# Routing rewritten: choices by tile, one strided operation, blocks by rounding, expert 0 first, first gathers borderless; condition loaded first

## What is computed

```
c_act = silu(c)
mod = c_act @ w_mod + b_mod                       # 1024 -> 6 x 1024
sh1, sc1, gt1, sh2, sc2, gt2 = split(mod, 6)
h = rms_norm(x, g_norm1) * (1 + sc1) + sh1
u = h @ w_in ; attention over q, k, v ; conv branch over ga, gb
x = x + gt1 * (concat(attn, conv) @ w_out)
h2 = rms_norm(x, g_norm2) * (1 + sc2) + sh2
x = x + gt2 * hier_moe(h2)

hier_moe: grp = argmax over 4 group logits; top 2 of the 8 expert logits of that group
          weights = softmax(top 2) * softmax(group logits)[grp]
          the 1024 assignments sorted by expert, each expert padded to whole blocks of rows
          y = (silu(xb @ w_gate[e]) * (xb @ w_up[e])) @ w_down[e]   for each block
```

## Time and profile before

| | us |
|---|---|
| median of three runs (2045.68, 2050.49, 2052.24) | 2050.49 |
| the profiled execution | 2045.59 |
| its span | 2044.0 |
| PE busy in the span | 1875.2 (92%) |
| DVE busy | 1243.2 (61%) |
| ACT busy | 1005.9 (49%) |

### The profile page before, as it was taken

The page is one execution under the profiler, slowest core; times in us unless marked ns, Lnnn a source line. Parts: engine busy times, 40 slices in busy tenths (PEclk is TensorE's granted clock), DMA queues, the critical chain, the costliest instruction groups (busy, mean ns, idle before and its releaser), DMA issues. The chain is left out here.

```text
span 2044.0 us, 28612 instructions
## 1 busy us (share of the span) xinstructions
PE 1875.2 (92%) x10635; PEld 1540.7 (75%) x10635; DVE 1243.2 (61%) x1673; ACT 1005.9 (49%) x1461; POOL 118.1 (6%) x159
## 2 busy tenths in 40 slices
PE   3999895899999999993799989989999989999997
PEld 1883443788888888883785569988999779899886
DVE  3865555799998999996435546734225554544333
ACT  3423421788887888884455653345332333322322
POOL 1001000111111111111100000000000000000000
PEclk8999996899999999997899999989999999999999
DMA  8856912899999999997111011112233113232321
GB/s 301 277 187 186 374 35 103 314 384 387 388 377 379 388 393 396 387 364 251 49 52 43 1 42 42 42 42 84 83 104 104 63 52 104 85 102 84 123 83 41
DMA packets 116101, 372.67 MB, mean 182 GB/s; under 512 B 8175, under 2 KB 70917, under 8 KB 102695
## 3 DMA queue, kind: packets, MB, share of 16 engines
q1 hardware_dynamic: 108566, 348.08, 46.5%
q0 software_dynamic: 7072, 23.13, 3.4%
q10 hardware_dynamic: 370, 0.14, 0.0%
HBM read 333.09 MB, written 33.82 MB: 180 GB/s over the span
## 5 line engine op out<-in xcount | busy, mean ns | idle before, releaser
L1444 DVE TENSOR_TENSOR parts_memory<-fixed,parts_memory 128x1024 fp32r<-128x1024 f32 x384 | 443.1, 1219 | 47.9 <-ACT parts_memory L1396 46.4
L1396 ACT ACTIVATE parts_memory<-fixed 128x1024 fp32r<-128x1024 f32 x384 | 375.0, 1066 | 38.7 <-DMA fixed<-in_w_exp_gate_dram 37.9
L1658 PE MATMUL psum<-parts_memory 128*128 128x256 f32 (+3 forms) x1136 | 345.6, 304 | 9.5 <-PEq L1875 3.3
L1659 PE MATMUL psum<-parts_memory 128*128 128x256 f32 (+3 forms) x1136 | 341.8, 301 | 0.0
L1660 PE MATMUL psum<-parts_memory 128*128 128x256 f32 (+3 forms) x1136 | 341.7, 301 | 0.0
L1557 DVE TENSOR_TENSOR parts_memory<-fixed,parts_memory 128x1024 fp32r<-128x1024 f32 x139 | 166.9, 1221 | 217.4 <-ACT parts_memory L1549 217.3
L1658 PEld LDWEIGHTS psum<-parts_memory 128*128 128x128 f32 x1136 | 216.6, 191 | 19.3 <-DVE parts_memory L1557 4.6
L1659 PEld LDWEIGHTS psum<-parts_memory 128*128 128x128 f32 x1136 | 216.8, 191 | 7.0
L1660 PEld LDWEIGHTS psum<-parts_memory 128*128 128x128 f32 x1136 | 216.7, 191 | 6.9
L1658 PE MATMUL psum<-mix_parts,parts_memory 128*128 128x256 f32 (+2 forms) x664 | 206.4, 311 | 4.7 <-PEq L2579 4.0
L1326 PE MATMUL psum<-parts_memory,token_parts 128*128 128x512 f32 x512 | 206.1, 403 | 2.8 <-DVE parts_memory L1444 2.8
(11 more groups left out here) (422 smaller groups left out, 2888.2 us busy)
## 6 DMA issues: line engine op xcount, KB each, us to landing
fixed<-in_w_exp_gate_dram SPq DMA_DIRECT2D x32, 2048.0 KB
fixed<-in_w_exp_up_dram SPq DMA_DIRECT2D x32, 2048.0 KB, 10.5
fixed<-in_w_exp_down_dram SPq DMA_DIRECT2D x32, 2048.0 KB, 9.9
fixed<-in_w_in_dram SPq DMA_DIRECT2D x36, 1024.0 KB, 5.4
expert_rows<-fixed SPq DMA_DIRECT2D x8, 2560.0 KB, 25.5
fixed<-in_w_mod_dram SPq DMA_DIRECT2D x8, 2048.0 KB, 10.8
fixed<-in_w_ffn_up_dram SPq DMA_DIRECT2D x11, 1024.0 KB, 5.3
fixed<-in_w_ffn_gate_dram SPq DMA_DIRECT2D x11, 1024.0 KB, 5.3
```

Source lines behind the costliest of these rows:

```text
L1396: act.activation(weights[:, 0, piece, :], ring[:, s, q * PIECE:(q + 1) * PIECE], ACT.Copy).then_inc(high_ok, 1)
L1444: dve.tensor_tensor(out, src, high_part.bitcast(F32), ALU.subtract).then_inc(done, 1)
L1658: pe.matmul(out, x(0), w(0), start=start, stop=False)
L1659: pe.matmul(out, x(0), w(1), start=False, stop=False)
```

## The change

- The condition c is loaded by itself and first; PE turns it alone, so that silu(c) and the products with it wait for c and no longer for all parameters. The parameters are turned behind the fourth `mod`, and ACT copies them behind the root.
- `idle_products` are products of constants into a bank that nobody reads: one behind each of the last four `mod(k)`, two behind the turn of the mod rows, three behind the rank products and three at the end of the routing.
- In the attention stage ACT writes sh2 and sc2 with their channels already permuted, so that only one operation by half tile, x times sc2, reads with a stride; it no longer needs the norm. The root takes scale and eps with it (`eps_col`), which removes DVE's variance step, and the norm comes in with sh2 in one fused operation by half tile.
- PE's order puts route(t-1) into the middle of the second half of a tile's mix and turn(t-1) behind the first half; DVE chooses for tile t-1 (`choose`) between the two halves of tile t.
- Group logits are padded to eight with -1e30, which saves a copy. Blocks come by rounding: adding 1.5 * 2^30 in fp32 rounds to a multiple of 128. The one-hot is written in halves. Weights of the choices, block counts and the list of experts are computed behind the table.
- The first block is always expert 0's (`least` gives it at least 128 rows), so its weights are loaded without waiting for a result: down at the start of the stage, gate and up behind the last mix.
- The first two gathers move from the expert stage into the routing stage, right behind the table, with all 128 rows and no branch. In the expert stage ACT and DVE split the first gate weights ahead of the first tokens.

The diff, cut to its core:

```diff
@@ input_projection
             pe.wait_ge(built, 4)
-            pe.wait_ge(params, 16 * n_params)
-            for i, (rows, n) in enumerate(((rows1, N_COLS + 16), (rows2, TAPS * CM), (rows3, 3 * FM))):
-                pe.transpose(psum[:, i, 0:n], rows[0:n, :], ident[0:n, 0:n]).then_inc(cols_ps, 1)
+            pe.wait_ge(c_in, 16)
+            pe.transpose(psum[:, C_BANK, 0:KT], c_rows[0:KT, :], ident[0:KT, 0:KT]).then_inc(c_ps, 1)
             pe.wait_ge(c_ready, 2)
...
-            for k in range(3, KT):
+            mod(3)
+            pe.wait_ge(params, 16 * n_params)
+            for rows, n, at in ((rows1, N1, 0), (rows2, N2, N1), (rows3, N3, N1 + N2)):
+                pe.transpose(psum[:, COLS_BANK, at:at + n], rows[0:n, :], ident[0:n, 0:n]).then_inc(cols_ps, 1)
+            pe.wait_ge(built, 7)
+            for k in range(4, KT):
                 mod(k)
+                idle_products(g, pe, IDLE_BANK, 1)
...
+            idle_products(g, pe, IDLE_BANK, 2)
...
+            act.dma_start(c_rows[0:KT, :], a["c"].rearrange("a (k p) -> (a k) p", p=P)).then_inc(c_in, 16)
...
+def idle_products(g, pe, bank, count):
+
+    for _ in range(count):
+        pe.matmul(g["psum"][:, bank, :], g["ident"], g["constants"], start=True, stop=True)
@@ attention_and_conv, ACT
             def mod_rows(i):
-                act.wait_ge(rows_ps, i + 1)
-                act.activation(modacc[:, 2048 + 512 * i:2560 + 512 * i], psum[:, S_BANK + i % 2, :], ACT.Copy).then_inc(rows_sb, 1)
+                row, half = divmod(i, 2)
+                out, src = modacc[:, 2048 + 512 * i:2560 + 512 * i], psum[:, S_BANK + half, :]
+                if row in (1, 2):
+                    act.wait_ge(rows_ps, 2 * row + 2)
+                    out = modacc[:, 2048 + D * row:2048 + D * row + D].rearrange("p (k n) -> p n k", k=KT)[:, 64 * half:64 * half + 64, :]
+                    src = src.rearrange("p (n k) -> p n k", k=KT)
+                else:
+                    act.wait_ge(rows_ps, i + 1)
+                act.activation(out, src, ACT.Copy).then_inc(rows_sb, 1)
@@ output_and_routing, SP and POOL
+            load_expert(g, sp, EXPERT_SLOTS[2], 0)
...
-            sp.wait_ge(first_ok, 1)
-            e = sp.value_load(first_expert, min_val=0, max_val=EXPERTS - 1)
             for slot in EXPERT_SLOTS[:2]:
-                load_expert(g, sp, slot, e)
-            for i in range(2):
-                sp.wait_ge(stored[i], 32)
+                load_expert(g, sp, slot, 0)
...
+            for i in range(2):
+                pool.wait_ge(stored[i], 32)
+            pool.wait_ge(cleared, 1)
+            pool.wait_ge(index_ok, 1)
+            for j in range(2):
+                pool.indirect_dma_start(
+                    out=g["ring"][:, 3, j * D:(j + 1) * D], out_offset=None, in_=dram["h2"],
+                    in_offset=bass.IndirectOffsetOnAxis(ap=first_index[:, j:j + 1].bitcast(U32), axis=0)
+                ).then_inc(g["tokens_in"][j], 16)
@@ PE
-            for t in range(TT):
-                for n in range(2):
-                    i = 2 * t + n
-                    if i >= 4:
-                        pe.wait_ge(taken, i - 3)
-                    mix(i, range(4 if i < 4 else 0, KT)).then_inc(ready, 1)
-                if t:
-                    turn(t - 1)
-                if t > 1:
-                    route(t - 2)
-            route(TT - 2)
+            for i in range(2 * TT):
+                t, n = divmod(i, 2)
+                if i >= 4:
+                    pe.wait_ge(taken, i - 3)
+                    mix(i, range(4))
+                if t and n:
+                    route(t - 1)
+                mix(i, range(4, KT)).then_inc(ready, 1)
+                if t and n == 0:
+                    turn(t - 1)
             turn(TT - 1)
             route(TT - 1)
...
+            idle_products(g, pe, 0, 3)
+            for i in range(PAIRS8):
+                if i in (0, TT):
+                    pe.wait_ge(hot_ok, 1 + i // TT)
...
+            idle_products(g, pe, 0, 3)
@@ DVE
+            def half_rows(t, n):
...
+                step(dve.tensor_tensor(h2_part, strided(res[:, t, cols], KT), sc2.rearrange("p (k n) -> p k n", k=KT)[:, :, part],
+                                       ALU.mult))
+            def normed(t):
+                dve.wait_ge(root, t + 1)
+                step(dve.reciprocal(rstd[:, t:t + 1], rstd[:, t:t + 1]))
+                for half in range(2):
+                    c = slice(512 * half, 512 * half + 512)
+                    dve.scalar_tensor_tensor(out=h2[:, t % 2, c], in0=h2[:, t % 2, c], scalar=rstd[:, t:t + 1], in1=sh2[:, c],
+                                             op0=ALU.mult, op1=ALU.add).then_inc(h2s, 1)
...
+            for t in range(TT):
+                half_rows(t, 0)
+                if t:
+                    choose(t - 1)
+                half_rows(t, 1)
+                normed(t)
+            choose(TT - 1)
+            dve.wait_ge(rank_ps, 1)
+            step(dve.tensor_scalar(counted, psum[:, 7, P:P + EXPERTS], 63.5, BIG, ALU.add, ALU.add))
+            step(dve.scalar_tensor_tensor(out=filled, in0=counted, scalar=-BIG, in1=least, op0=ALU.add, op1=ALU.max))
+            step(dve.tensor_tensor_scan(ends[:, 1:], ones[:, 0:EXPERTS], filled, 0.0, ALU.mult, ALU.add))
+            step(dve.tensor_tensor(where, psum[:, 7, 0:P].rearrange("p (t n) -> p t n", t=TT),
+                                   ends[:, 0:EXPERTS].unsqueeze(1).to_broadcast([P, TT, EXPERTS]), ALU.add))
...
@@ experts
                 if not (isinstance(b, int) and b == 1):
                     sp.wait_ge(low_ok, down_done(b - 2))
-                load_expert(g, sp, DOWN, eb)
+                    load_expert(g, sp, DOWN, eb)
...
-            gather(0, 0, 0)
-            gather(1, 1, 0)
             n = run(pool, body)
...
+            high(0, 0, gate_at, GATE, 16)
             take_x(0, 0)
             n = run(act, body)
...
+            low(0, 0, gate_at, GATE)
             take_x(0, 0)
             n = run(dve, body)
```

339 lines of the change are left out of this document (165 added, 174 removed).

## The result

The changed kernel takes 2033.54 us (median of six runs, 2027.40 to 2037.26), the kernel before 2050.45 in the six runs beside it: ratio 0.9918, 95% interval 0.9901 to 0.9935, 16.9 us. The forecast was 2025, so the sign and most of the mechanism hold, and 8.5 us of the gain are missing. The profiled execution took 2031.47 us with a span of 2029.8, against 2045.59 and 2044.0.

| mark (us) | before | after | earlier |
|---|---|---|---|
| P, first projection product | 47.58 | 38.75 | 8.8 |
| R, start of the routing stage (SP's first request) | 254.51 | 246.50 | 8.0 |
| S, first work of the expert stage | 354.41 | 345.79 | 8.6 |
| W, first projection product of the second transformer block | 987.95 | 971.67 | 16.3 |
| end of the span | 2044.0 | 2029.8 | 14.2 |

What follows compares the result with a forecast made beforehand. PE was taken as the bound, with reachable gaps at the start and around slice 7. Terms -10.7+0.6-7.2-6.9 = -24.2 gave 2021.4 from the profiled execution, taken as 2025 because the runs' median lay higher; own range 2018 to 2030.

Steps and rivals of the forecast that it cites:

- Start: Kernel start: c loaded first brings w_mod's eighth block and the projections earlier, clock held: -10.7 us, bounds -7.8 and -15.
- Rival (b): Start: c lands with the other parameters at 20.5, so the start gains about 1: -14, 2036 us; chance 0.06.
- Attention: End of attention: PE's next row product waits one ACT copy longer for permuted gate rows: +0.6 us, between 0 and 1.5.
- Routing: the step that failed: Routing stage: shorter choices, positions and table products let the expert stage begin 7.2 us sooner; bounds -2 and -9.
- 3.2 us until the barrier: Routing's end: weights, expert list, pair count and exponentials behind the table's reading take 3.2 us instead of 0.4: +2.8.
- the last mix was to end 5.4 us later: Routing, PE's order: turns and routes inside the mix delay its last product, ending at 322.4 rather than 317.0.
- The 4.8 of the positions: Routing, behind the ranks: DVE's eleven steps up to the one-hot take 4.8 us instead of 8.0: -3.1.
- the 1.8 of the tables' clock: Routing: table products cost 1.8 us more if the idle products don't hold the clock.
- First block: Expert stage's start: early gathers and weights end PE's wait and low clock at the second gate: -6.9 us, bounds -3 and -9.
- (a): Start and routing: idle products don't hold the clock, table products read 0.50 again: -18.3, 2031 us; chance 0.17.
- (c): Experts: expert 0 always gets a block; if no token chose it, 34 blocks run: +11, 2061 us; chance 0.02.
- (d): Experts: transfers, not PE, are the bound, so earlier requests gain 7 more: 2018 us; chance 0.06.

Runs made afterwards that it cites:

- e6: Kernel before with only the changed kernel's new start; attention, routing and experts as before: 2037.63 us, ratio 0.9939 to before.
- e7: Changed kernel without the start's idle products, those of the routing kept: 2038.82 us, one run.
- e4: Changed kernel with eight idle products ahead of the first tile's turn and sixteen ahead of the last one's: 2041.00 us, ratio 0.9956 to before.
- e8: Changed kernel with two idle products ahead of the first tile's turn and four ahead of the last one's: 2027.92 us, one run.
- e12: Changed kernel with two and four idle products ahead of first and last turn, and first two gathers moved into the expert stage: 2023.66 us, ratio 0.9871 to before.
- e5: Changed kernel with the gate rows copied plainly by ACT, each half as it stands, and DVE reading them with a stride: 2035.78 us, one run.
- e1: Changed kernel with the first two gathers issued as GpSimd's first work of the expert stage: 2028.29 us, ratio 0.9891 to before.
- e2: Changed kernel with the two first gathers replaced by plain reads of the same size on SyncE's queue: 2033.44 us, one run.
- e9: Changed kernel with the two first gathers replaced by plain reads of the same size on GpSimd's own queue: 2029.02 us, one run.
- e3: Changed kernel with eight idle products ahead of the first tile's turn: 2035.16 us, one run.
- e10: Changed kernel with all four tiles' choices made after the last tile's logits: 2040.59 us, one run.
- e11: Changed kernel without the routing's idle products, three ahead of the table products and three at the stage's end: 2037.51 us, one run.

## Why the prediction was right, and where not
Its steps, in the profiled executions:

| step | predicted | measured |
|---|---|---|
| start and attention, to R | -10.1 | -8.0 |
| routing, R to S | -7.2 | -0.6 |
| first block, S to W | -6.9 | -7.7 |
| behind W | 0 | +2.1 |
| sum | -24.2 | -14.2 |

- **Start.** Right. The eighth block was to be read near 33 (33.42) and the projections to start near 38 (38.75). e6 puts the whole step at -11.1 to R, of which 0.6 are chance, so -10.5 where -10.7 was said; the clock's part is 1.4 (e6), and 1.3 was said. The eighth block was requested at 21.6 and landed at 33.1; in e7 it was requested at 24.0, 2.4 us later, and landed at 33.4, so that its time follows from what was asked for before it and not from its own request. The Trainium skill (DMA: Bandwidth & Descriptors, "Two DMAs through the same engine are not ordered") says that descriptors within one queue of a DMA engine start in order; the traces agree. Rival (b) falls, c was turned at 3.4 us.
- **Attention.** The wait was named, its size was too small: +0.6 said, with bounds of 0 and 1.5. Old and new copies have to be compared at the same clock in the attention. At 1.00, e6 with the old copies takes 204.9 us from P to R, and e4, e8 and e12 take 205.9 to 206.3; at 0.97, e5 takes 205.15 and five traces of the changed code 206.4 to 206.6. So the price is 0.9 to 1.5, the upper half of the bounds. The copy itself grows from 0.61 to 0.95 us when it writes with a stride, which I had not priced. The profiled execution is also a late one at R, with the clock at 0.94 in the attention; with this same code R came at 244.3 to 246.6. Of the 2.1 us missing up to R, some 0.8 are the copies, 0.8 that clock, and 0.6 P, which came at 38.75 and not at 38.2.
- **Routing: the step that failed.** Two terms of it. First, "3.2 us until the barrier", and behind it nothing but the barrier's own time. The last work did end 3.2 us behind the reading of the table (337.9 to 341.1), but the stage didn't end with it: it waited until POOL's two gathers had landed, 4.65 us instead of 0.3 (e1, e2, e9). So the gathers that were issued early to be under way during the barrier made the barrier last as long as they did. Second, the order of PE: the last mix was to end 5.4 us later (counted from R) and ended 8.3 later. I had the stall of the first tile about right (0.8 more said; PE stood 2.05 us against 1.69 before, and with the clock held it waits another 0.34 for ACT ahead of the route, as e3 shows), but not what the clock takes behind it: 2.9 us until mix 4 (e3, e8), and 1.7 to 4.6 in the seven traces with this stand. Together they cost 7.2 us, where 6.6 are missing; the other terms came out a little better than said.
- The other terms of the routing came as said: choices 2.65 (2.7), ranks to the reading of the table 8.2 (8.5), last work 3.2 behind it. The 4.8 of the positions are a slip: their terms add up to 4.3 with the first half of the one-hot, 5.0 with both, and 4.3 was measured (331.46 to 335.76). That three tiles' choices are free is shown by e10 (8.5 us if they aren't), the 1.8 of the tables' clock by e11 (1.7 at the products, 1.4 at S). In e11 the clock stays at 0.50 from the end of the mix into the expert stage; with the idle products it is back at 1.00 ahead of the table.
- **First block.** Right: -6.9 said, -7.7 measured to W. No wait ahead of the second gate group, and its stretch is at the full clock. e6, with the old routing and expert stages, takes 632.9 from S to W, the changed kernel 625.9. Which of the edits brings this (early gathers, the order of the splits, expert 0 first) is not shown: no run takes the last two out, and e1, with late gathers, has 628.0.
- **Rivals.** (a) The clock is up at the table products (1.98 us), so it falls as it was put; but the same cause struck at two places where no idle products stand. (c) falls, W would come later. (d) falls: from the second gate group (14.1 us earlier) to W the gain grows by 2.2, of which 1.6 are the low clock of 382 to 385 us that is gone, and not by 7.
- Behind W, 2.1 us were lost by the same code; the clock in the first 80 us there was 0.96 instead of 0.99. That I take for chance: over the fourteen traces this stretch takes 1056.1 to 1064.2, and the kernel before has the shortest. The medians (16.9) are the better measure of the gain than the two profiled executions (14.2).

## What to carry to other kernels
Before a transfer is moved ahead of a stage's end, ask on whose queue it is: in this kernel GpSimd's had to be empty before the stage could end, SyncE's had not. A stall has two prices, its own length and the low clock behind it; two idle products in a 2 us stall gave back 2.9 us (1.7 to 4.6, by the trace they are set against), but they must be sized by the duration that a trace shows for one of them, since four times too many turned the gain into a loss of 7.5. And where identical code varies by 8 us between executions, judge an edit by the distance between two marks of the trace, and at the same granted clock: the price of the copies reads as 1.7 us when e6 is set against the middle of all traces, and as 0.9 to 1.5 when only stretches at the same clock are compared.

## What the hardware showed that I had not expected
- The end of the routing stage waited for DMAs outstanding on GpSimd's queue, indirect or plain: the next stage began 4.65 us behind the last work with two gathers, 2.9 with two plain reads, 0.3 with the same reads on SyncE's queue.
- ScalarE's copy of 128x512 out of PSUM takes 0.95 us instead of 0.61 when its output has a stride of 128 elements, and VectorE's three-operand step 1.10 instead of 0.71 when one operand is read with a stride of eight. Its product of two operands takes 1.08 us with one of them strided and 1.09 with both (e5).
- After a stand of 2.05 us TensorE fell to 1.2 GHz, not during the stand but behind it: 0.6 us into the next work in the changed kernel, some 2.6 us into it in e9, where the turn still took 1.32 us. In the kernel before and in e6 a stand of 1.69 at the same place had no such effect. When it fell and how long it stayed low differs between executions: from the first turn to mix 4 it is 6.7 us with the clock held, and 8.41 to 11.29 in the seven traces with this stand.
